# Sum of squares of the differential outputs by two rounded passes instead of one in full precision

## What is computed

```
def _rmsnorm(x, g, eps=EPS):
    x32 = x.astype(jnp.float32)
    y = x32 * lax.rsqrt(jnp.mean(x32 * x32, axis=-1, keepdims=True) + eps)
    return (y * g.astype(jnp.float32)).astype(x.dtype)

def _diff_attention(q, k, v, lq1, lk1, lq2, lk2, subln_g, lam_init):
    ...
        attn = p[:, :, 0] - lam * p[:, :, 1]
        return jnp.einsum('bhqk,bkhe->bhqe', attn.astype(v.dtype), v)

    o = _sweep(block, s).reshape(b, s, N_DIFF, DIFF_V)
    o = _rmsnorm(o, subln_g, SUBLN_EPS) * (1.0 - lam_init)
    return o.reshape(b, s, W_A)
```

## Time and profile before

| what | us |
|---|---|
| median of 3 runs | 2498.05 |
| lowest and highest | 2497.83, 2498.51 |
| span of the profiled execution, first to last instruction | 2495.6 |
| median less that span | 2.45 |
| PE busy | 2476.7 |
| DVE busy | 2131.8 |
| ACT busy | 1523.2 |

### The profile page before, as it was taken

One profiled execution on the slowest core, in us unless ns is written; L12 is line 12 of the kernel. 1 busy time (PEld: TensorE's weight loads), 2 busy tenths in 40 slices (PEclk: granted clock), 3 DMA queues, 4 the chain that ended last, 5 costly groups with the idle time before them and its releaser, 6 DMA issues.

```text
span 2495.6 us, 49294 instructions
## 1 busy us (share of the span) xinstructions
PE 2476.7 (99%) x15824; PEld 2248.2 (90%) x15824; DVE 2131.8 (85%) x3881; ACT 1523.2 (61%) x3059; POOL 4.4 (0%) x13
## 2 busy tenths in 40 slices
PE   9999999999999999999999999999999999999998
PEld 7999888888889989998889998888888998899987
DVE  8999868888898779998799997788888986799986
ACT  7666447777764456664466654578777454566643
POOL 0000000000000000000000000000000000000000
PEclk9999999999999999999999999999999999999999
DMA  4323331211222232223322233212211322233333
GB/s 165 110 101 103 109 102 62 66 60 60 68 94 101 94 102 102 101 101 119 110 94 101 101 106 122 81 65 60 68 60 60 110 94 102 93 102 109 109 110 102
DMA packets 65258, 235.74 MB, mean 94 GB/s; under 512 B 7232, under 2 KB 7488, under 8 KB 65088
## 3 DMA queue, kind: packets, MB, share of 16 engines
q1 hardware_dynamic: 65088, 233.64, 27.8%
HBM read 231.51 MB, written 2.10 MB: 94 GB/s over the span
## 4 chain that ended last, share of the span: by engine, by line
PE 91%; DVE 5%; issue 2%; ACT 1%; DMA 1%; DVEq 0%; SPq 0%; ACTq 0%
PE ps L665 28%; PE ps L666 28%; PE ps L667 28%; PE ps L906 2%; DVE w_lo L1782 1%; PE ps L837 1%; PE ps L826 1%; PE ps L880 1%; PE ps L879 1%; PE ps L828 1%; DVE area L1782 1%; DMA w_raw<-weights 1%; PE ps L893 0%; PE ps L843 0%; PE ps L895 0%
## 5 line engine op out<-in xcount | busy, mean ns | idle before, releaser
L1136 ACT ACTIVATE w_hi<-w_raw 128x512 fp32r<-128x512 f32 (+1 forms) x876 | 627.6, 723 | 475.2 <-PE ps L667 232.8
L1782 DVE TENSOR_TENSOR w_lo<-w_raw,w_hi 128x512 fp32r<-128x512 f32 (+1 forms) x876 | 701.7, 807 | 115.3 <-ACT w_hi L1136 99.4
L665 PE MATMUL ps<-u_hi,w_hi 128*128 128x256 f32 (+1 forms) x2432 | 787.3, 324 | 2.1 <-DVE w_lo L1782 1.7
L667 PE MATMUL ps<-u_hi,w_lo 128*128 128x256 f32 (+1 forms) x2432 | 780.8, 321 | 0.0
L666 PE MATMUL ps<-u_lo,w_hi 128*128 128x256 f32 (+1 forms) x2432 | 780.5, 321 | 0.0
L666 PE MATMUL ps<-area,w_hi 128*128 128x256 f32 (+1 forms) x1764 | 580.9, 329 | 0.0
L665 PEld LDWEIGHTS ps<-u_hi,w_hi 128*128 128x128 f32 x2432 | 463.3, 190 | 36.9 <-DVE w_lo L1782 3.0
L667 PEld LDWEIGHTS ps<-u_hi,w_lo 128*128 128x128 f32 x2432 | 463.2, 190 | 34.8
L666 PEld LDWEIGHTS ps<-u_lo,w_hi 128*128 128x128 f32 x2432 | 463.5, 191 | 32.7 <-issue 1.4
L665 PE MATMUL ps<-area,w_hi 128*128 128x256 f32 (+1 forms) x1400 | 480.1, 343 | 0.4 <-DVE h L1804 0.4
L667 PE MATMUL ps<-area,w_lo 128*128 128x256 f32 (+1 forms) x1400 | 477.6, 341 | 0.0
(11 more groups left out here) (187 smaller groups left out, 2908.6 us busy)
## 6 DMA issues: line engine op xcount, KB each, us to landing
w_raw<-weights SPq DMA_DIRECT2D x435, 512.0 KB, 3.7
h<-x SPq DMA_DIRECT2D x4, 512.0 KB, 7.5
out<-scratch_whole SPq DMA_DIRECT2D x8, 256.0 KB, 2.2
scratch_whole<-const_b SPq DMA_DIRECT2D x1, 512.0 KB, 9.8
scratch_whole<-const_r SPq DMA_DIRECT2D x1, 320.0 KB, 9.2
scratch_whole<-lambdas SPq DMA_DIRECT2D x1, 256.0 KB, 2.8
cst<-const SPq DMA_DIRECT2D x1, 137.0 KB, 7.8
par<-params SPq DMA_DIRECT2D x1, 94.0 KB, 2.5
```

The lines of the kernel that those rows point to most:

```text
L665: pe.matmul(dst, hi, x_hi, start=start, stop=False, **kw)
L667: return pe.matmul(dst, lo, x_hi, start=False, stop=stop, **kw)
L1136: return act.activation(dst, src, ACT.Copy)
L1782: return dve.tensor_tensor(dst, src, hi_part.bitcast(F32), ALU.subtract)
```

## The change

The square of the differential output is no longer summed by one float32 product with `ones`. ACT makes a rounded copy of the square after it (`o_sq_hi`, in the unused seventh piece of `w_hi`), DVE forms the rest (`o_sq_lo`, in the scratch area), and PE sums the two with two rounded matmuls against `negones_r`. The sum comes out negative, so the scale in `output_rstd` changes its sign. The new DVE step stands between `qk_lo(2, 0, 0)` and `qk_lo(2, 2, 1)` in the head calls, and before `used(2)` and `split(2)` in the tail calls. `o_sq`, for which PE waits, is now signalled by DVE.

```diff
@@ -426,6 +426,7 @@
         acc = tile(7)
+        o_sq_hi, o_sq_lo = w_hi[:, (PIECES - 1) * SEQ:], scratch_r[:, 4 * SEQ:5 * SEQ]
@@ -496,6 +497,7 @@
         o_whole_set = sem("o_whole_set")
+        o_sq_hi_set = sem("o_sq_hi_set")
         o_sq = sem("o_sq")
@@ -910,7 +912,8 @@
             def diff_norm(bank=AUX):
                 pe.wait_ge(o_sq, c.next(o_sq))
-                pe.matmul(ps[:, bank, :], ones, tile(7), start=True, stop=True).then_inc(o_ms, 1)
+                pe.matmul(ps[:, bank, :], negones_r, o_sq_hi, start=True, stop=False)
+                pe.matmul(ps[:, bank, :], negones_r, o_sq_lo, start=False, stop=True).then_inc(o_ms, 1)
@@ -1473,12 +1476,14 @@
             def output_square():
                 act.wait_ge(o_mm, c.next(o_mm))
-                act.activation(tile(7), ps[:, OB, :], ACT.Square).then_inc(o_sq, 1)
+                act.activation(tile(7), ps[:, OB, :], ACT.Square).then_inc(act_done, 1)
+                act.wait_ge(act_done, c.next(act_done))
+                hi(o_sq_hi, tile(7)).then_inc(o_sq_hi_set, 1)
 
             def output_rstd(bank=AUX):
                 act.wait_ge(o_ms, c.next(o_ms))
                 act.activation(tile(7), ps[:, bank, :], ACT.Ln, bias=cst[:, C_EPS + 1:C_EPS + 2],
-                               scale=1.0 / (2 * HEAD)).then_inc(act_done, 1)
+                               scale=-1.0 / (2 * HEAD)).then_inc(act_done, 1)
@@ -2318,6 +2323,11 @@
+            def output_square_lo():
+
+                dve.wait_ge(o_sq_hi_set, c.next(o_sq_hi_set))
+                lo(o_sq_lo, tile(7), o_sq_hi).then_inc(o_sq, 1)
+
@@ -2389,6 +2399,7 @@
                     turned_lo(3)
                     qk_lo(2, 0, 0)
+                    output_square_lo()
                 qk_lo(2, 2, 1)
                 take(2, 1.0)
                 split(2)
```

More of the change, by code:

```diff
@@ L1777, in _ @@
                              rstd_set, gate_out, g_hi_set, qk_hi_set,
-                             v_hi_set, score_set, exp_set, log_set, pt_hi_set, o_rstd, o_norm, o_rest_set, o_hi_set,
+                             v_hi_set, score_set, exp_set, log_set, pt_hi_set, o_sq_hi_set, o_rstd, o_norm, o_rest_set, o_hi_set,
                              proj_mm, tail_read, prob_set, qk_set])
```

## The result

| | median us | range | runs |
|---|---|---|---|
| before | 2498.20 | 2497.83 to 2498.51 | 5 |
| changed | 2508.18 | 2507.98 to 2508.81 | 5 |

The changed kernel takes 1.004 times as long, with a 95% interval of 1.0029 to 1.0051: 10.0 us more where 10.5 were forecast. The profiled run took 2508.18 us and has a span of 2506.4, 10.8 more than before.

A forecast was written before the change was run, and what follows sets the result against it. PE was taken to bound the kernel. Six head calls at +1.41 us and two tail calls at +1.03 sum to 10.5 us, giving 2508.6 us (+0.42%), with 8 in 10 between 2505.8 and 2511.

The forecast's parts named there:

- What bounds the kernel: Whole kernel: PE is busy for 2476.7 of 2495.6 us, so only its own sequence moves the end.
- The saving: PE's sum of the square: two rounded matmuls for one full-precision pass, 0.39 us a call, 3.1 us over 8.
- The chain of added steps: ACT copy, DVE subtraction and hand-overs between square and pair: the pair cannot start until 1.46 us after the square.
- The head call: Six calls in the tile loop: PE waits 0.87 before the pair and 0.82 before the scores, net +1.41 us each.
- The choice between 0.61 and 0.70: DVE start spacing around qk_lo in head calls: 0.70 taken, giving +1.41 us a call; one at 0.61 gives 1.32.
- The tail call: Two diff_norm(SB0) calls: PE waits for the added steps, +1.03 us each, with no second wait.
- Parts costed at nothing: Later split(2), take(2), output_rstd, the changed sign and the semaphore: covered or free, cost 0.
- rival D: Head calls: PE waits for DVE's later take(2) or weight split, about +1 us each, 2514.6 us; chance 0.03.
- The sum: Whole kernel: 8.46 + 2.06 = 10.5 us; span 2506.1 plus an unchanged 2.45 around it, 2508.6 us.
- A: Head calls: only the wait before the pair shows, 0.59 us each, total 5.6, 2503.7 us; chance 0.05.
- B: All calls: added steps hidden under PE's projection blocks, only the saving left, -3.1, 2494.9 us; chance 0.05.
- C: PE's clock falls behind the waits, about 2.8 us lost in each of 8 calls, +22, 2531 us; chance 0.02.

The follow-up runs named there:

- e3: Changed kernel without the rest of the square: ACT writes the square rounded, PE sums it twice at half the scale; 2495.44 us beside 2497.92 before.
- e5: As e4, with output_rstd moved among the stick logarithms and the rest of the square elsewhere in scratch; 2496.96 us beside 2497.74 before.
- e1: Changed kernel with DVE's new subtraction moved behind qk_lo(2, 2, 1) in the six head calls; 2502.64 us beside 2497.92 before.
- e2: Changed kernel with all added steps kept but unused, PE summing the square in one float32 pass; 2506.82 us beside 2497.92 before.
- e4: As e1, with PE computing the head calls' stick scores first and summing the square behind them; 2500.75 us beside 2497.74 or 2497.92 before (+2.8).
- e8: As e5, with PE summing the square in the two tail calls behind the first two product blocks; 2497.10 us beside 2497.74 before.
- e9: Head calls as in e5, the two tail calls with one float32 pass as in the kernel before; 2495.14 us beside 2498.03 before.
- e6: Changed kernel with DVE forming the rest of the square twice; 2517.09 us beside 2497.74 before.
- e11: Changed kernel with DVE forming the rest of the square three times; 2525.51 us beside 2498.03 before.
- e10: Changed kernel in its two tail calls only, head calls summing in one pass as before; 2499.82 us beside 2498.03 before.

## Why the prediction was right

*What bounds the kernel*: right. PE's busy time did not move with the span; only its waits did.

*The saving*: 0.39 a call forecast; 0.37 to 0.38 measured in head calls (e3, e5), nothing in tails (e3). The 8 x 0.39 = 3.1 us was never to be had in full.

*The chain of added steps*: 1.46 us forecast from the end of the square to the pair, 1.45 measured (458.24 to 459.69). Copy 0.63 for 0.64, subtraction 0.69, hand-overs 0.03, 0.04 and 0.06.

*The head call*: +1.41 forecast, +1.43 to +1.44 measured, and in both pieces (0.85 for 0.87 before the pair, 0.86 for 0.82 before the scores): the scores start 3.51 us after the weighted values where the working has 3.49. e1 and e2 show the reason and not only the size: `qk_lo` queued behind the new subtraction sets the scores' start, and the pair's own wait counts nothing beside it. The choice between 0.61 and 0.70 for the first `qk_lo` was right: it starts 0.73 behind the subtraction, while in e4, where a full-height instruction follows instead, the distance is 0.61 (timeline of DVE in e4):

```profile
458.58 0.69 DVE L1788 TENSOR_TENSOR scratch<-scratch_whole,w_hi 128x512 fp32r<-128x512 f32 x1 [0.28 <-ACT w_hi L1140]
459.19 0.69 DVE L2259 SCALAR_TENSOR_TENSOR scratch_whole<-ps,rstd 128x512 f32<-128x512 f32 x1
```

The rule of the Trainium skill ("VectorE: DVE Perf Modes", section "Two Vector instructions with no wait between them") that was weighed there agrees with both rows.

*The tail call*: +1.03 forecast, +1.00 at the second product and 0.9 to 1.0 over the whole tail. The size was right and its account incomplete, and that they agree is partly luck. The prediction followed PE's wait alone. The chain goes on from the pair's sum through `output_rstd` to DVE's normalisation, 4.20 us behind the square for 3.20, and e2, e3 and e8 show that this alone is enough to set the tail. PE and DVE happen to be late by the same 1.0 us.

*Parts costed at nothing*: right in the head calls. No wait before unit 4 or 5 appears; rival D has no row. In the tail the path through `output_rstd` and the normalisation was given no cover at all, and it has none. One reading was off without effect: the 0.9 us in 2 calls of the earlier trace rows is idle time of the weight loads (PEld) of L913; PE itself waits about 0.15 us there, as the same paragraph says from the earlier trace rows.

*The sum*: 10.5 forecast, 10.8 in the spans, 10.0 in the medians. The 2.45 us that were taken for the part around the span, and as unchanged, are in no run: it is 2.09 to 2.21 before and 1.78 to 1.85 changed. That the forecast of 2508.6 lies within 0.4 of 2508.18 is therefore partly luck: the span came out 0.3 longer than the 2506.1 forecast and the part around it 0.65 shorter than taken.

*The rivals*: A was made real by e1, and costs what was worked out for it (0.58 a head call for 0.59). B would have needed cover. e5 supplies it in the head calls, and there the saving is all that is left, -0.38 each, 2.3 us for six; that e9's median of -2.9 comes near B's -3.1 is chance, since B counts eight calls. C is the one that was weighed too lightly. In the changed kernel the clock stays at 1.00 through every head call, so the forecast was not touched. But the 1.27 us wait that spoke against it in the trace was a single one, and e6 shows that 0.6 us more a call is enough for three of eight to fall. The Trainium skill ("TensorE: Matmul & The Clock Gate", section "HAM oscillation — how this bites in real kernels") describes falls behind longer waits for DMA, at every one of them. e6 and e11 agree that waits between matmuls put the clock back, but show it with waits of 1.30 and 0.70 us, and not at every call. The price taken for a fall, 2.8 us, was too high: about 1.55 was measured.

## What to carry to other kernels

When a step is given to an in-order engine, ask first what stands behind it in that queue and who waits for that: here the instruction queued behind the new one cost more than the new one's own consumer. A saving on the bounding engine that is paid with steps on other engines must come with cover for them; with the same steps, order alone moved the result from +10.0 to -0.8 us (e5), and with the two tail calls left in one pass it was -2.9 (e9). And before moving one engine's wait in a delayed chain, follow what the chain's end releases on the other engines: in the tail the late sum went on through ACT and DVE, and filling PE's wait brought nothing.

## What was not expected of the hardware

The granted clock of TensorE: behind two waits of 1.30 and 0.70 us with the pair between them, or one of 2.0 us in a tail, PE ran for about 3 us at its lower level, in three of eight calls of e6; with the first wait 0.6 us longer, in six of eight of e11; with 0.69 and 0.69, or 1.38 in a tail, in none of the changed kernel's. It is not settled what decides it in a given call.

The start scatters. The 18 warming products took 7.00 us in the kernel before and 5.91 to 7.16 in others with the same instructions there, and the first head call's square started at 456.92 (e3) to 457.72 (e10), which doesn't follow the edits. Up to about 0.8 us of any comparison of two single profiles of this kernel is that. The two numbers don't go together either: in e8 the warming products are 1.25 us shorter than in the changed kernel, and the next matmul starts at 10.11 for 10.15, because it waits for the weight rest. The changed kernel's timeline of PE:

```profile
3.10 7.16 PE L1080 MATMUL ps<-area 128*128 128x512 f32 x18 [3.10 <-issue]
```

The same in e8:

```profile
3.09 5.91 PE L1083 MATMUL ps<-area 128*128 128x512 f32 x18 [3.09 <-issue]
10.11 0.51 PE L668 MATMUL ps<-u_hi,w_hi 128*128 128x512 f32 x1 [1.12 <-DVE w_lo L1791]
```
